# A modulation block moved into each head's wait, and the end of the expert stage rebuilt, in a two-layer diffusion step

## The reference

```python
def rmsnorm(x, g):
    xf = x.astype(jnp.float32)
    y = xf * lax.rsqrt(jnp.mean(xf * xf, axis=-1, keepdims=True) + EPS)
    return (y * g.astype(jnp.float32)).astype(x.dtype)
...
    for i in range(DEPTH):
        j = i // N_MIXERS
        sh1p, sc1p, g1p, sh2p, sc2p, g2p = modulation(c_ctx, w_ada[i], b_ada[i])
        ...
        hp = rmsnorm(xp, norm_g[i, 0]) * (1.0 + sc1p) + sh1p
        ...
        xp = xp + g1p * yp
        ...
        hp = rmsnorm(xp, norm_g[i, 1]) * (1.0 + sc2p) + sh2p
        ...
        xp = xp + g2p * hier_moe(hp, ...)
```

## Time and profile before

| | |
|---|---|
| three timed runs | 1233.75, 1238.2, 1239.68 us (median 1238.2) |
| profiled execution, its own time | 1235.03 us |
| span of its instructions | 1233.2 us |
| mean granted TensorE clock | 0.982 of full |
| busy share of PE, DVE, ACT, POOL | 92%, 35%, 18%, 11% |

### The profile page before, as it was taken

How to read it: one execution, slowest core, us unless ns; L and a number is a source line. 1 busy time by engine, 2 the same in 40 slices (tenths; PEclk the granted TensorE clock), 3 DMA queues, 4 the chain that set the end, 5 groups by cost and what they waited for, 6 DMA issues and landing times.

```text
span 1233.2 us, 20046 instructions
## 1 busy us (share of the span) xinstructions
PE 1132.9 (92%) x8612; PEld 677.2 (55%) x8612; DVE 428.2 (35%) x1108; ACT 225.2 (18%) x523; POOL 136.0 (11%) x219
## 2 busy tenths in 40 slices
PE   4999999998899999999988899989989899999885
PEld 1666666665444666666654444434545766666552
DVE  2255555555612440100003755307843420000007
ACT  2210111101211411110100311116622321011010
POOL 0333343333100000000003100000000000000012
PEclk9999999999999999999999999999989999999998
DMA  9982444435932348999999923236751279999993
GB/s 348 305 269 87 139 138 138 138 138 196 394 118 78 137 189 332 427 425 424 426 428 405 338 69 136 85 133 226 274 205 68 77 303 427 425 425 425 427 421 141
DMA packets 97601, 317.08 MB, mean 257 GB/s; under 512 B 3792, under 2 KB 38912, under 8 KB 81120
## 3 DMA queue, kind: packets, MB, share of 16 engines
q1 hardware_dynamic: 90160, 298.05, 63.0%
q10 hardware_dynamic: 5248, 10.97, 2.3%
q0 software_dynamic: 2096, 6.67, 1.5%
HBM read 304.67 MB, written 11.01 MB: 256 GB/s over the span
## 4 chain that ended last, share of the span: by engine, by line
issue 70%; PE 21%; DMA 4%; DVE 2%; POOL 1%; ACT 0%; SPq 0%; POOLq 0%; DVEq 0%
PE bank L790 11%; PE bank L799 4%; DMA ring<-in_w_ada 2%; PE bank L477 2%; DMA ring<-expert_rows,moe_row 2%; PE bank L815 2%; DVE ring L1679 1%; PE bank L871 1%; PE bank L483 1%; PE bank L824 0%; PE bank L882 0%; PE bank L864 0%; DVE uT L1677 0%; ACT hg_raw L1096 0%; DVE hg_kf L1773 0%
## 5 line engine op out<-in xcount | busy, mean ns | idle before, releaser
L672 PE MATMUL bank<-ring,xn 128*64 128x256 f32 x1536 | 174.3, 385 | 11.8 <-DMA ring<-in_moe_w_up 9.0
L672 PEld LDWEIGHTS bank<-ring,xn 128*64 128x64 f32 x1536 | 111.6, 139 | 77.0 <-issue 11.6
L790 PE MATMUL bank<-uT,ring 128*128 128x384 f32 x384 | 135.1, 496 | 0.0
L984 PE MATMUL bank<-ring,uT 128*128 128x512 f32 x288 | 126.4, 594 | 1.6 <-issue 1.3
L1667 DVE TENSOR_TENSOR moe_hh<-xn,bank 128x256 f32<-128x256 f32 x32 | 13.5, 421 | 308.0 <-ACT xn L1164 307.9
L2033 POOL TENSOR_TENSOR moe_flag<-con 128x1 f32<-128x1 f32 x2 | 0.4, 193 | 846.9 <-DMA expert_rows<-xn 846.9
L661 PE MATMUL bank<-moe_g,moe_h 128*128 128x128 f32 x768 | 93.7, 280 | 0.0
L661 PEld LDWEIGHTS bank<-moe_g,moe_h 128*128 128x128 f32 x768 | 90.0, 195 | 5.4 <-issue 5.4
L790 PEld LDWEIGHTS bank<-uT,ring 128*128 128x128 f32 x384 | 69.3, 190 | 42.5 <-issue 2.4
L984 PEld LDWEIGHTS bank<-ring,uT 128*128 128x128 f32 x288 | 53.7, 190 | 65.6 <-issue 65.6
L688 PE MATMUL bank<-ring,xn 128*64 128x512 f32 x384 | 85.0, 595 | 1.6 <-DMA ring<-in_moe_w_down 1.6
(11 more groups left out here) (269 smaller groups left out, 1292.7 us busy)
## 6 DMA issues: line engine op xcount, KB each, us to landing
ring<-in_w_ada SPq DMA_DIRECT2D x24, 2048.0 KB, 10.0
ring<-in_moe_w_gate SPq DMA_DIRECT2D x24, 2048.0 KB, 18.1
ring<-in_moe_w_up SPq DMA_DIRECT2D x24, 2048.0 KB, 22.3
ring<-in_moe_w_down SPq DMA_DIRECT2D x24, 2048.0 KB, 27.4
ring<-in_hgrn_w_in SPq DMA_DIRECT2D x32, 512.0 KB, 6.8
moe_ring<-in_moe_w_gate SPq DMA_DIRECT2D x8, 2048.0 KB, 22.5
moe_ring<-in_moe_w_up SPq DMA_DIRECT2D x8, 2048.0 KB, 24.1
moe_ring<-in_moe_w_down SPq DMA_DIRECT2D x8, 2048.0 KB, 20.7
```

The lines of the kernel that those rows point to most:

```text
L672: last = mm(bank[2 + e][64 * g:64 * g + 64, 256 * part:256 * part + 256], m["xe"][:, k, 64 * e:64 * e + 64], cols(slot)[:, k, 256 * g:256 ...
L790: last = mm(to[:, 0:TOK], w[:, k, f, :], uT[:, k, :], start=(k == 0), stop=(k == KC - 1))
L984: last = mm(bank[b % 2][:, :], uT[:, k, t * P:(t + 1) * P], cols(slot)[:, k, :], start=(k == 0), stop=(k == KC - 1))
```

## The change

It has three parts.

Heads: PE issues `ada_block` after level 6 and before the wait for the level's operands, into bank 5 (of old after the head's output, into bank 6). POOL makes `kd` of a head as soon as the products that read the previous one are done; only `qab` waits for `o_done`.

End of the expert stage, in both layers: the last pair's two down matrices come in halves of 512 columns (four loads of 1 MB), `down` starts on the first halves, and PE places their rows (`first_halves`) between the two halves of `down`. `collect` waits for the first halves too. Tile 1's fetched rows are added on PE (`fetched_rows`, by the diagonals `rw`). Tiles 0 and 2 are summed on DVE; POOL adds nothing more. Two `keep_busy(2, 512)` stand where `keep_busy(6, 512)` stood, and `keep_busy(8, 512)` ahead of layer 1 is gone.

Norm of layer 1: tile 0 is squared, rooted and scaled inside the pass (`next_root`, `next_norm`), PE transposes tiles 1 and 2 within the first two products of the projection, and the load of its first weights waits for the fetched rows of tile 2. The means are no longer made by DVE: ACT's root takes 1/count as scale and EPS as bias, here and in all other norms.

```diff
+            def last_down(n, p):
+
+                for half in range(2):
+                    here = slice(512 * half, 512 * half + 512)
+                    for e in range(2):
+                        slot, use = expert_slot(n, PAIRS - 1, 4 + e)
+                        if half == 0:
+                            sp.wait_ge(*expert_free(n, PAIRS - 1, 4 + e, p))
+                        src = a["moe_w_down"][n, 2 * (PAIRS - 1) + e].rearrange("(k p) n -> p k n", p=P)
+                        sp.dma_start(down_rows(slot).rearrange("p g j n -> p (g j) n")[:, :, here], src[:, :, here])\
+                            .then_inc(S[n]["down_half"] if half == 0 else full[n][slot], 16)
...
+                if b == 0:
+                    sp.wait_ge(S[0]["rows2"], count * 32)
+                elif slot == SLOT_ORDER[0][0]:
                     sp.wait_ge(S[0]["added"], count * T + (T - 1))
+                else:
+                    sp.wait_ge(used[0][slot], count * USES + uses_before[0][slot])
...
                     if i == PAIRS - 1:
-                        keep_busy(6, 512)
-                    rows_of = [down_rows(weights_in(i, 4 + e)) for e in range(2)]
+                        keep_busy(2, 512)
+                        pe.wait_ge(s["down_half"], at_pass[0] * 32 + 32)
+                        rows_of = [down_rows(expert_slot(n, i, 4 + e)[0]) for e in range(2)]
+                    else:
+                        rows_of = [down_rows(weights_in(i, 4 + e)) for e in range(2)]
...
+                        if half == 1 and i == PAIRS - 1:
+                            first_halves(it)
+                            keep_busy(2, 512, 7)
+                            for e in range(2):
+                                weights_in(i, 4 + e)
...
+                def first_halves(it):
+
+                    pe.wait_ge(s["wc_ready"], at_pass[0] + 1)
+                    pe.wait_ge(s["oe_ready"], it * 2 + 1)
+                    last_pair(0, 0, True, True).then_inc(s["last_mm"], 1)
+                    last_pair(1, 0, True, False)
+                    last_pair(2, 0, True, True)
+
+                def fetched_rows(half):
+
+                    here = slice(512 * half, 512 * half + 512)
+                    for j, rows in enumerate((m["own"], second_rows[n])):
+                        done = mm(bank[LAST_BANKS[1][half]][:, :], m["rw"][:, j, :], rows[:, 1, here],
+                                  start=False, stop=(j == 1))
+                    return done
...
+                    last_pair(0, 1, True, True).then_inc(s["last_mm"], 1)
+                    last_pair(2, 1, True, True).then_inc(s["last_mm"], 1)
+                    last_pair(1, 1, True, False)
+                    pe.wait_ge(s["rows1"], p * 32 + 32)
+                    fetched_rows(0)
+                    fetched_rows(1).then_inc(s["last_mm"], 1)
...
+                pe.wait_ge(hg["free_b"], (h + 1) * PAIRED)
+                ada_block(b, turn + 1, 5)
                 pe.wait_ge(hg["qa_f"], h * 8 + 8)
                 pe.wait_ge(hg["qa_b"], h * 8 + 8)
                 need(pe, 0, "mod_cols", h + 4)
@@ -883,8 +937,6 @@
...
                 last.then_inc(hg["o_done"], 1)
-
-                ada_block(b, turn + 1, 6)
 
...
-            keep_busy(8, 512)
-            for t, banks in enumerate(((6, 4), (2, 3), (5, 7))):
-                need(pe, 1, "xn_ready", t + 1)
-                turn_tile(1, "xT_done", xn, t, banks)
+            def turn_features(t):
+
+                pe.wait_ge(norm_dve, count + t)
+                turn_tile(1, "xT_done", xn, t, LAST_BANKS[t])
...
                     for k in range(KC):
+                        if m == 0 and k == 4:
+                            need(pe, 1, "uT_dve", t + 1)
                         last = mm(bank[b % 2][:, :], uT[:, k, t * P:(t + 1) * P], cols(slot)[:, k, :],
                                   start=(k == 0), stop=(k == KC - 1))
+                        if b < 2 and k == (6, 4)[b]:
+                            turn_features(b + 1)
...
+            def next_root(t, done):
+
+                A(xn[:, t, :], x[:, t, :], ACT.Square, accum_out=stat[:, 0, t:t + 1]).then_inc(norm_act, 1)
+                act.wait_ge(norm_act, done + 1)
+                root_of(stat[:, 2, t:t + 1], stat[:, 0, t:t + 1], D).then_inc(norm_act, 1)
...
+            need(act, 1, "mod_ready", 2)
+            modulate(1, "xT_done", "uT_act", 0, LAST_BANKS[0][0])
+            modulate(1, "xT_done", "uT_dve", 0, LAST_BANKS[0][1], 1)
+            for t in (1, 2):
                 act.wait_ge(S[0]["added"], count * T + t)
-                square(1, "squares", t, MOE["h"])
-            root(1, "mean_ready", "root", 0)
-            root(1, "mean_ready", "root", 1)
-            act.wait_ge(S[0]["added"], count * T + 2)
-            square(1, "squares", 2, MOE["h"])
+                next_root(t, count * 2 + (2 * t - 2))
...
+            def next_norm(t, done):
+
+                dve.wait_ge(norm_act, done * 2 + (2 * t + 2 if t == 0 else 2 * t))
+                v.reciprocal(stat[:, 0, 8 + t:9 + t], stat[:, 2, t:t + 1]).then_inc(S[0]["root_done"], 1)
+                dve.wait_ge(S[0]["root_done"], done + (1 if t == 0 else t))
+                v.tensor_scalar(xn[:, t, :], x[:, t, :], stat[:, 0, 8 + t:9 + t], None, ALU.mult).then_inc(norm_dve, 1)
...
                         own_row, other = m["own"][:, t, :], second_rows[n][:, t, :]
                         dve.wait_ge((s["rows0"], s["rows1"], s["rows2"])[t], p * 32 + 32)
...
+                        await_step(step(v.tensor_scalar(own_row, own_row, m["hw"][:, 0, t:t + 1], None, ALU.mult)))
+                        await_step(step(v.scalar_tensor_tensor(other, other, m["hw"][:, 1, t:t + 1], own_row, ALU.mult, ALU.add)))
+
+                    def gated_rows(t):
+
+                        other = second_rows[n][:, t, :]
+                        await_step(step(v.tensor_tensor(other, other, gates[:, SIDE[t], :], ALU.mult)))
+                        await_step(step(v.tensor_tensor(x[:, t, :], x[:, t, :], other, ALU.add)))
+
+                    def last_added(t, half):
+
+                        here = slice(512 * half, 512 * half + 512)
+                        other, last_pair = second_rows[n][:, t, here], bank[LAST_BANKS[t][half]][:, :]
+                        dve.wait_ge(s["last_mm"], p * LAST_MM + (2 + half, 5, 4)[t])
+                        if t == 2:
+                            await_step(step(v.tensor_tensor(other, other, last_pair, ALU.add)))
+                            last_pair = other
+                        await_step(step(v.tensor_tensor(other, last_pair, gates[:, SIDE[t], here], ALU.mult)))
+                        added = v.tensor_tensor(x[:, t, here], x[:, t, here], other, ALU.add)
+                        if half == 1:
+                            added.then_inc(s["added"], 1)
+
+                    rows_summed(0)
+                    gated_rows(0)
+                    last_added(0, 0)
+                    last_added(0, 1)
+                    rows_summed(2)
+                    if n == 0:
+                        next_norm(0, p)
+                    for t in range(1, T):
+                        last_added(t, 0)
+                        last_added(t, 1)
...
-                pool.wait_ge(hg["o_done"], h)
+                if h > 0:
+                    pool.wait_ge(hg["lev_f"], (h - 1) * 8 + 1)
                 pool.wait_ge(hg["zb_ready"], h + 1)
                 g.tensor_tensor(HG["kd"][:, :], HG["kf"][:, b, :], kb, ALU.add).then_inc(hg["kd"], 1)
+                pool.wait_ge(hg["o_done"], h)
                 g.tensor_tensor(HG["qab"][:, :], q, fb, ALU.mult).then_inc(hg["qa_b"], 1)
...
                     pool.wait_ge(s["oe_out"], p * (16 * WRITES) + 16 * WRITES)
+                    pool.wait_ge(s["down_half"], p * 32 + 32)
                     g.tensor_tensor(m["flag"][:, 1:2], ones[:, 0:1], ones[:, 0:1], ALU.mult)
...
-                    for t in range(T):
-                        pool.wait_ge(s["placed"], p * PLACED + (LAST_WEIGHTED + 3 * t + 3))
-                        g.tensor_tensor(x[:, t, :], x[:, t, :], second_rows[n][:, t, :], ALU.add).then_inc(s["row_added"], 1)
```

199 lines of the change are left out of this document (96 added, 103 removed).

## The result

The changed kernel takes 1216.57 us, the median of 4 runs (1213.33 to 1217.25); the kernel before took 1236.64 beside it. The ratio is 0.985, 95% interval 0.982 to 0.988: faster by 20 us. The profiled execution took 1217.25 us, span 1215.4, 17.8 us under that of before.

What follows compares the result with a forecast made beforehand. PE, busy 92%, was taken to bound the kernel. Gains 13.9 (heads) + 6.7 (layer 0's stage end) - 0.4 (kernel's end) = 20.2 us off 1235.03 gave 1214.8; median placed 1.2 above, 1216, range 1207 to 1225.

Steps and rivals of the forecast that it cites:

- Heads: All heads: moved block and early `kd` gain 12.5 us at six transitions, 0.1 at the seventh, 1.3 behind head 7: 13.9 us.
- each transition: From head to head: block and wait go, 2.27 us less, block stands 0.2 too long in the gap: net 2.1 us.
- The seventh: Transition into head 7: PE would wait for the second early block's load, landing after 8.2 us; gain only 0.1 us.
- The last term: Behind head 7, block no longer between output and gate projection: gain 1.3 us, between 0.5 and 2.1.
- Stage's end: End of layer 0's expert stage: projection's third tile at 703.2 against 709.92, gain 6.7 us, bounds 3 to 9.2.
- Kernel's end: End of layer 1's expert stage: DVE's last addition ends at 1229.4 against 1228.98, 0.4 us lost; bounds -2 to +3.
- (1): Heads: level 0 of the next head waits for DVE, 1 us a head instead of 2.1: 1222 us; chance 0.12.
- (2): Expert stage's end: late weights or rows, or a costlier PE branch, leave gain 0 to 2: 1222 us; chance 0.12.
- (3): Start of layer 1's projection: PE's clock falls with fillers gone, 5 us lost: 1221 us; chance 0.06.
- (4): Expert stages, both layers: first halves land late, PE waits 16.8 us in each: 1250 us, slower; chance 0.03.
- (5): Heads: `kd` not ready in time because POOL waits on something else, gain 0.5 us each: 1226 us; chance 0.05.
- the page's load time: Head 7's block load at 6.8 us for 2 MB instead of 8.2: seventh transition gains 1.5 us, sum 21.4.

Runs made afterwards that it cites:

- block_end: Changed kernel with the block's 16 products back at the head's end on bank 6, `kd` product still early: 1225.53 us, 0.993 of the kernel before.
- kd_late: Changed kernel with the `kd` product again behind the wait for the head's output, block still in the gap: 1221.42 us, 0.989 of the kernel before.
- heads_only: Kernel before with only the heads' edits (block in the gap on bank 5, early `kd` product): 1223.13 us, 0.990 of the kernel before.
- no_fill_qkv: Changed kernel without the fillers between the last halves in both layers, first query load waiting for its slot only: 1210.82 us, 0.981 of the kernel before.
- early_later: Changed kernel with early block 1's product and the turn of its result one level later in head 7: 1213.6 us, 0.983 of the kernel before.
- no_fill: Changed kernel without the two fillers between the expert stage's last halves, in both layers: 1212.46 us, 0.979 of the kernel before.
- after: The changed kernel itself, first measurement, against the kernel before: 1216.57 us, 0.985; its profiled execution took 1217.25 us.
- fill_layer0: Changed kernel without the two fillers in layer 1's expert stage alone, layer 0's kept: 1210.54 us, 0.980 of the kernel before.

## Why the prediction was right

**Time.** Forecast 1216 in 1207 to 1225; measured 1216.57 and 1213.05. The sum of 20.2 us stands against 17.8 and 20.8 us between the two spans and that of before. The mechanism is the one forecast; that the first median hit within 0.6 us is luck: the second lies 3.5 us lower, and the profiled execution gained 3.0 us less in the heads than forecast, and 0.6 us more at the stage's end.

**Heads: 13.9 us, measured 10.9 in the profiled execution and 12.4 on average** (three ends without the block's move at 325.0, ten with it at 312.6). The 2.1 us of each transition is 2.11 in the trace, and both reasons were shown: the block fills the gap (`block_end`), POOL's early product removes the next wait (`kd_late`). The seventh: block 1 gained 11.65 us in all, where I had 12.6: its load was issued 12.1 us earlier and took 8.8 us to its use, where I had 8.2 for landing. The last term, 1.3 us behind head 7, held: from the output's last products to the gate projection it was 4.10 us before and is 2.55 now (320.64 to 324.74, 311.31 to 313.86), with DVE taking the four early blocks as I had said; less the 0.2 us that the block stands too long in its gap that is 1.3 us. What the sum left out is head 7 between these places: from block 1 to the output's last products it took 2.1 us more than before, beyond those 0.2, and over the ten executions some 1.1 us on average. I had seen one wait in head 7 and put the rest at nothing. There are more: the late instruction (1.15 us in the kernel before, up to 4.01 us now), late loads of blocks 2 or 3 once block 1 waits less, and the clock behind each. The two executions with the shortest heads, 13.7 and 14.2 us gained (`heads_only`, `no_fill_qkv`), had no late instruction; `early_later` had none either, but waited for its loads. By the Trainium skill, DMA: Bandwidth & Descriptors, anatomy of one DMA, this load would take an estimated 6.8 us; the page's fit is for DMAs that GpSimd issues, and this one is SP's. The rows show 8.8 us (277.11 to 285.91) with the DMAs at 0.85, and the row was the better price.

**Stage's end: 6.7 us, measured 7.3.** In the old frame (12.12 us added) the steps came so: first halves landed 660.6 (659.8), placing done 670.2 (670.0), fetched rows done 682.7 (682.5), tile 0 ready 682.0 (682.0), projection 686.0 (686.5), third tile 702.6 (703.2). (In brackets what I had forecast.) The branch was 0.94 us of issue, where I took 1.90 over from before; 0.3 us of it went to the way from PE's transposes to the projection. The gathers were faster (5.3 us from the second one's issue to DVE's use, where I had 8.9), but nothing hung on that. That the weights are just there was right too: asked for sooner, in `no_fill`, they are waited for. Shown by itself is the share of the halves; how the rest divides between the norm inside the pass, the transposes inside the projection and PE's products on fetched rows is argued from the rows, since no run undoes one of them alone.

**Kernel's end: -0.4, measured -0.35.** The table's last stretch is the same to 0.1 us, so here the forecast and the result are both near nothing.

**Rivals.** (1) DVE as the heads' floor: no, it takes level d 1.1 us ahead. (2) Nothing gained at the stage's end: no; whole matrices alone would have taken 3.9 us of the 7.3. (3) Half clock: it varies between executions of the same code, and costs less than I had. Eight executions have the changed stage of layer 0 as it is. Four of them (42.7 to 43.2 us in the table) ran through it at full clock, three ran the first filler, or its end and the products behind it, at half clock (44.4), one the projection's start (44.8): 1.7 us each time, not 5. So this rival comes true in part in half of the executions. In head 7 block 1 waited 2.1 to 3.4 us for its load in nine traces with both edits, and in seven of them it then took 2.55 to 3.64 us instead of 1.92. The rule that I weighed, in the Trainium skill, TensorE: Matmul & The Clock Gate, on oscillation in real kernels, that waits for a DMA bring the clock down, fits these seven rows and not the other two; the cases in the stage, behind the same idle time each way, no row here explains. (4) The first halves late: no, they landed 0.5 us before PE's filler began. (5) `kd` late: no; `kd_late` measured its price, 1.2 us a transition. Two sums in my text were off: with the page's load time the sum is 21.6 and not 21.4, and rival 1 leaves 13.7 and not 14.3; nothing above hangs on either.

**Open.** Why the packet of instructions in head 7 comes up to 4 us too late. Up to 278 us there are 25 such packets, with the DMAs at 0.49 on average, and PE has no gap behind any of them. And the stretch between the stages (487 to 491 us in kernels that don't differ there) cost this execution 1.7 us against before's 489.5; the twelve other kernels lie between 486.9 and 490.7 us there, so I take it for spread.

## What to carry to other kernels

Fill a wait with work that stands in the open elsewhere, but look what that work was covering: here moving the block alone would have bared the `kd` product and kept less than half of the gain, and the early `kd` alone gained nothing. When a stage becomes faster, its last unit meets the loads at their own pace; there part of the gain goes, and in head 7 shifting a request only moved the wait. Give the streams (half matrices, gathered rows, next weights) the order in which the compute engine asks for them: each of three such orders was worth 1 to 4 us in its stage. And fillers that cover no wait cost nearly their length: 3.6 us at this kernel's end.

## What the runs showed of the hardware that was not expected

- An instruction can be missing for 0.8 to 4.0 us in the same head of a program, with the DMA engines at 0.86 of their time (`after`, 295.7 to 298.7) as well as at 0.13. In all eleven traces that have the wait its end lies 2.0 to 2.7 us behind a packet of the instruction queue.
- After a wait of 2.2 us (`down` whole) sixteen records took 5.35 us instead of 3.65, at a granted clock of 0.68. But with the same 0.69 us of idle time ahead of it the first filler took 1.98 us in some executions and 3.1 to 3.6 in others: here is one of the latter, layer 0 of `fill_layer0` (granted clock 0.55).

```profile
647.66 3.49 PE L613 MATMUL bank<-con 128*128 128x512 f32 x4 [0.69 <-ACT xn L1238]
```

- The end of the heads is at 310.6 to 315.4 us in ten executions whose code is the same there but for two small moves; where block 1 waited 0.6 us for its load or not at all, three agree within 0.7.
